# Hybrid encoder step on one core: projection begun inside its norm, gates spread over its tiles, FFN's first half turned between the second's products

## Chip, cores and metric

One core of a Trainium2 chip. The metric is the device time of the whole step in microseconds, of the one core that runs it. Every product is made in three passes of split float32 operands (high x high, high x low, low x high).

## What is computed

The reference, cut to what matters (x is 2048 prompt rows and 32 sample rows of 1024; D_FF is 2816):

```python
h = _rmsnorm(x, norm1_g)
z = h @ w_in                                   # 1024 x 3096
fq, fk, fv, fl, gq, gk, gv, gg, gr = split(z)  # 512 512 512 8 256 256 512 16 512
logf = log_sigmoid(fl + b_forget)
glog = log_sigmoid(gg @ w_gate2 + b_gate2) / 16
fox_o = softmax(fq.fk/8 + cumsum(logf) differences, causal) @ fv   # prompt; sample over 4096 cached rows
gla_o, S = gated linear attention in chunks (gq, gk, gv, cumsum(glog))
x = x + [fox_o, rmsnorm(gla_o) * silu(gr)] @ w_out
h = _rmsnorm(x, norm2_g)
x = x + (silu(h @ w_gate) * (h @ w_up)) @ w_down
y = _rmsnorm(x, final_norm_g)
```

## The kernel before

Each stage is a scope of its own with its SBUF tiles, semaphores and a barrier of all engines at its end: `project`, `gates`, `fox_prompt`, `fox_sample`, `gla`, `merge`, `ffn`. The engines' programs are written by hand, in order, one function per engine, with semaphores between them. Loads and stores go through SP's queue.

`project` (L133). The 2080 rows are 20 x tiles of 104. For each, ACT squares (L288) and takes the root (L292), DVE scales by its inverse and the gain (L348), PE turns eight 104x128 pieces (`turn_x`, L393), ACT copies the turned tile as high half (L297) and DVE subtracts it for the low half (L355). When all 20 are in `hT`, PE runs over 25 weight tiles of 128 columns: 8 column tiles, 16 row tiles and at the end the narrow one (8 forget gates and 16 gate ranks, run 128 wide). A weight tile takes 5 blocks of 416 rows, a block 24 products (8 depths x 3 passes, L405). ACT copies each block out (L314). Row tiles (k, v, GLA's v and its output gate) are turned back in groups of four 104-row pieces (`turn_rows`, L416): three groups after block 3, two after block 4, each after ACT's copy and before DVE's (L369). The column tiles are stored to `zT`, the row tiles to `new_k`, `new_v`, `zrow`.

`gates` (L452) begins when all that is stored. It reads the narrow tile back, makes the gate product (`gg @ w_gate2`, L552), takes min, Abs, Exp and Ln for the log sigmoids, sums along time with scans, sums the cached forget gates (L585 to L595), turns and stores `pbias`, `new_f`, `kbias`, `kb_split`, `gsum`. Nothing of the fox stage is loaded before its end.

`merge` (L1584) ends for each row tile with the second norm, whose turned rows `hT_m` are copied half by ACT (L1730), half by DVE (L1772) and stored as `h2T`.

`ffn` (L1832) takes the rows in two halves of 10 tiles (1040 rows, blocks of 4, 3 and 3 tiles). A half has 22 steps of 128 hidden columns; step u makes gate and up products of its columns (`gate_up`, 24 matmuls each per block, L2126) and, between them, the down products of the step before (`downs`, 12 matmuls a slot, six slots, L2141). DVE adds each down product to `yacc` (`adds`, L2061). The silu is exp on ACT (L2018), + 1, reciprocal and product on DVE (L2073 to L2077). ACT and POOL split the weights (L1998, L1957) and h (`hi_h`, `lo_h`, L2005, L1962; `hraw` holds two tiles). After a half's last down products, `final` (L2161, L2093, L2039, L2104) turns `yacc` back, adds x, norms and stores it, row tile by row tile, and POOL clears `yacc`; no product stands between.

Of the kernel before, what the change touches and what calls it, by code (L numbers as in the profile page):

```python
# [109 lines left out]
def fill_identity(pool, ident, filled):  # L110
# [10 lines left out]
TCOLS = [C_Q + P * n for n in range(4)] + [C_GQ + P * n for n in range(4)]  # L121
RCOLS = ([C_K + P * n for n in range(4)] + [C_V + P * n for n in range(4)]
         + [C_GV + P * n for n in range(4)] + [C_GR + P * n for n in range(4)])
NTT, NTR = len(TCOLS), len(RCOLS)
NWT = NTT + NTR + 1
R_Q, R_GQ, R_GK, R_K, R_F, R_GG = 0, 512, 768, 1024, 1536, 1544
XB = 4
NB = 5
BLK = NTOK // NB
TPB = BLK // TT  # L130


def project(nc, d):  # L133
    with ExitStack() as ctx:
# [4 lines left out]
        work = sb("work", [P, SEQ])  # L139
        xn = work[0:TT].rearrange("p (b c) -> p b c", b=2)  # L140
        zhi = work[:].bitcast(F32R)
        zlo = sb("zlo", [P, SEQ])
# [7 lines left out]

        xin = zs[0:TT].rearrange("p a t -> p (a t)")[:, 0:XB * D].rearrange("p (b c) -> p b c", b=XB)
        zr = sb("zr", [TT, NT, P])
        ps = psum("ps_project")
        x_in = [sem(f"x_in{b}") for b in range(XB)]
# [13 lines left out]
        def half_tile(n):  # L168

            return n if n < 4 else n - 4  # L170

        X_CREDIT = 2
        B_CREDIT = 2 * NB
        R_CREDIT = 2

        @block.sync
        def _(sp):
            for b in range(2):
                sp.sem_inc(t_stored[b], 16)
            sp.sem_inc(r_stored, 48)  # L180
            sp.sem_inc(halves_stored, 32)
            w = d["w_in"][0].rearrange("(k p) n -> p k n", p=P)

            def load_w(n):
# [3 lines left out]
                if n < NTT + NTR:  # L188
                    c = (TCOLS + RCOLS)[n]
                    sp.dma_start(wraw[:, b], w[:, :, c:c + P]).then_inc(w_come[b], 16)  # L190
# [4 lines left out]
            def load_x(t, b):  # L195
                sp.wait_ge(x_scaled, t + 1)
                sp.dma_start(xin[:, b], d["x_prompt"][0, bass.ds(t * TT, TT), :]).then_inc(x_in[b], 16)

            sp.dma_start(grow[:], d["norm1_g"].partition_broadcast(TT)).then_inc(g_in, 16)
            with sp.Fori(0, NT // XB - 1) as i:  # L200
                for b in range(XB):
                    load_x(XB * i + b, b)
            load_w(0)
            load_w(1)
            for b in range(XB - 1):
                load_x(NT - XB + b, b)

            sp.wait_ge(x_scaled, NT)
            sp.dma_start(xin[0:LAST_PROMPT, XB - 1], d["x_prompt"][0, (NT - 1) * TT:SEQ, :]).then_inc(x_in[XB - 1], 16)
            sp.dma_start(xin[LAST_PROMPT:TT, XB - 1], d["x_sample"][0]).then_inc(x_in[XB - 1], 16)  # L210

            def store_t(n, row, rows):
                sp.wait_ge(block_out, NB * (n + 1) + B_CREDIT)
                sp.dma_start(d["zT"][row:row + rows, :], zs[0:rows, n % 2]).then_inc(t_stored[n % 2], 16)

            def store_halves(n):
                part, j = divmod(half_tile(n), 4)
                sp.wait_ge(z_hi, half_tile(n) + 1)
                sp.dma_start(d["qk_hi"][part, j * P:(j + 1) * P, :], work[:]).then_inc(halves_stored, 16)
                sp.wait_ge(z_lo, half_tile(n) + 1)  # L220
                sp.dma_start(d["qk_lo"][part, j * P:(j + 1) * P, :], zlo[:]).then_inc(halves_stored, 16)

            def store_rows(n, prompt, sample, c):
                sp.wait_ge(rows_out, NB * (n - NTT + 1) + R_CREDIT)
# [10 lines left out]
            for n in range(NWT):  # L235
                if 1 <= n < NWT - 1:
                    load_w(n + 1)
# [379 lines left out]

# [1601 lines left out]
```

## Time and profile before

| | |
|---|---|
| runs | 3607.22, 3610.07, 3612.82 us; median 3610.07 |
| profiled execution | 3611.11 us, its span 3609.4 us |
| busy of the span | PE 3170.2 (88%), DVE 2241.3 (62%), ACT 1091.2 (30%), POOL 538.3 (15%) |
| mean granted clock of TensorE | 0.934 of full |
| chain that ended last, by line | PE L2126 27%, PE L2141 13%, loads of `yo` and `hraw` 2% |

The stages in time: norm and projection 0 to 700 us, gates to 768, fox prompt to about 1250, fox sample to about 1380, GLA to about 1670, merge to 1961, FFN to the end. Busy shares are averages over stages; what a change in a stage is worth is read from that stage. The time of the profiled execution is 1.7 us more than its span.

### The profile page before, as it was taken

The numbers are of one execution on the slowest core, as the hardware profiler recorded it, in microseconds if no ns is written. First come the engines' busy times: TensorE is split into PE (matmuls) and PEld (weight loads), VectorE is DVE, ScalarE is ACT, GpSimd is POOL, SyncE is SP. The second block draws the span as 40 slices with busy tenths as digits, with TensorE's granted clock in tenths as the row PEclk, the third lists the DMA queues.
The fourth block names the chain that finished last, engine by engine and source line by source line (L and its number), as shares of the span: only waits on it lengthen the run. The fifth ranks groups of instructions, "written<-read, shape, count | busy, mean of one in ns | idle before, by whom it ended". The sixth has DMA issues, their size and how long they took to land. (4 is left out here: it accounts for less than half of the span.)

```text
span 3609.4 us, 51369 instructions
## 1 busy us (share of the span) xinstructions
PE 3170.2 (88%) x19096; PEld 2924.1 (81%) x19096; DVE 2241.3 (62%) x3638; ACT 1091.2 (30%) x2163; POOL 538.3 (15%) x371
## 2 busy tenths in 40 slices
PE   5999999839999765664996999999997799999996
PEld 4999999728778644553774999999997799999995
DVE  5102111159999734995343678778776778778776
ACT  5211111138888622663222211111112211111112
POOL 0000000000000003661001322222124122222120
PEclk9999999859999976776998999999999899999997
DMA  4424312153342161222443311111112411111112
GB/s 111 164 71 160 104 53 70 31 110 65 71 95 53 31 217 40 83 80 94 127 142 125 90 46 46 41 46 46 46 56 78 119 46 44 43 46 46 46 48 81
DMA packets 249539, 281.24 MB, mean 78 GB/s; under 512 B 37729, under 2 KB 207089, under 8 KB 240137
## 3 DMA queue, kind: packets, MB, share of 16 engines
q1 hardware_dynamic: 248105, 275.71, 26.1%
q10 hardware_dynamic: 1344, 4.36, 0.6%
q8 instruction: 53, 0.87, 0.1%
q14 instruction: 37, 0.30, 0.0%
HBM read 196.33 MB, written 83.70 MB: 78 GB/s over the span
## 5 line engine op out<-in xcount | busy, mean ns | idle before, releaser
L2126 PE MATMUL ps_ffn<-h,wsp_n 128*128 128x312 f32 (+1 forms) x6336 | 1056.5, 323 | 42.2 <-POOL h L1962 29.5
L2126 PEld LDWEIGHTS ps_ffn<-h,wsp_n 128*128 128x128 f32 x6336 | 1017.4, 189 | 48.4 <-issue 38.4
L2061 DVE TENSOR_TENSOR yacc<-ps_ffn,yacc 128x312 f32<-128x312 f32 (+1 forms) x1056 | 495.2, 515 | 221.5 <-PE ps_ffn L2141 221.5
L405 PE MATMUL ps_project<-hT,wsp 128*128 128x416 f32 x3000 | 579.4, 353 | 3.2 <-DVE wsp L362 3.2
L405 PEld LDWEIGHTS ps_project<-hT,wsp 128*128 128x128 f32 x3000 | 561.4, 189 | 12.0 <-issue 5.0
L2141 PE MATMUL ps_ffn<-aT,dsp 128*128 128x312 f32 (+1 forms) x3168 | 545.0, 321 | 9.4 <-DVE yacc L2061 9.4
L2141 PEld LDWEIGHTS ps_ffn<-aT,dsp 128*128 128x128 f32 x3168 | 508.5, 188 | 12.2 <-issue 9.4
L2028 ACT ACTIVATE aT<-a 128x416 fp32r<-128x416 f32 x132 | 65.4, 495 | 1003.9 <-DVE a L2083 1003.9
L1957 POOL TENSOR_TENSOR wsp_n<-wraw_n,wsp_n 128x1024 fp32r<-128x1024 f32 x88 | 210.6, 2394 | 802.9 <-ACT wsp_n L1998 802.9
L2075 DVE RECIPROCAL silu<-silu 128x416 f32<-128x416 f32 x132 | 306.2, 2320 | 4.6
L2073 DVE TENSOR_SCALAR silu<-silu 128x416 f32<-128x416 f32 x132 | 221.9, 1681 | 49.9 <-ACT silu L2018 49.9
L1801 PE MATMUL ps_merge<-wsp_m,mT 128*104 128x512 f32 x960 | 227.9, 396 | 0.0
L941 DVE TENSOR_TENSOR pt<-ps_fox,pt 128x512 fp32r<-128x512 f32 (+1 forms) x320 | 194.5, 608 | 30.2 <-ACT pt L899 23.9
L362 DVE TENSOR_TENSOR wsp<-wraw,wsp 128x1024 fp32r<-128x1024 f32 x25 | 30.6, 1226 | 288.9 <-ACT wsp L305 288.9
L893 ACT ACTIVATE pexp<-ps_fox,ntop 128x512 f32<-128x512 f32 (+2 forms) x320 | 198.7, 621 | 36.2 <-DVE ntop L936 34.4
L1801 PEld LDWEIGHTS ps_merge<-wsp_m,mT 128*104 128x104 f32 x960 | 160.5, 169 | 58.8
L899 ACT ACTIVATE pt<-ps_fox 128x512 fp32r<-128x512 f32 (+1 forms) x320 | 171.0, 535 | 75.2 <-PE ps_fox L855 70.2
L928 DVE TENSOR_REDUCE tops<-ps_fox 128x1 f32<-128x512 f32 (+3 forms) x288 | 177.5, 617 | 26.2 <-PE ps_fox L821 24.9
L855 PE MATMUL ps_fox<-ident_f,pexp 128*128 128x128 f32 x1088 | 174.5, 276 | 2.3 <-DVE pt L941 1.6
L820 PE MATMUL ps_fox<-ka,qa 128*128 128x512 f32 (+2 forms) x320 | 127.2, 398 | 52.9 <-DMA kb<-kb_split 45.8
L1978 POOL TENSOR_TENSOR dsp<-draw,dsp 128x1024 fp32r<-128x1024 f32 x44 | 105.0, 2388 | 360.8 <-ACT dsp L2025 360.8
L855 PEld LDWEIGHTS ps_fox<-ident_f,pexp 128*128 128x128 f32 x1088 | 129.4, 144 | 26.7 <-DVE pt L941 5.8
(218 smaller groups left out, 3452.0 us busy)
## 6 DMA issues: line engine op xcount, KB each, us to landing
wraw_n<-in_w_gate_dram SPq DMA_DIRECT2D x44, 512.0 KB, 3.9
wraw_n<-in_w_up_dram SPq DMA_DIRECT2D x44, 512.0 KB, 3.8
draw<-in_w_down_dram SPq DMA_DIRECT2D x44, 512.0 KB, 3.6
zT<-zs SPq DMA_DIRECT2D x12, 1040.0 KB, 3.9
wraw<-in_w_in_dram SPq DMA_DIRECT2D x24, 512.0 KB
x<-x2s SPq DMA_DIRECT2D x20, 416.0 KB
h2T<-hT_m SPq DMA_DIRECT2D x20, 416.0 KB
hraw<-h2T SPq DMA_DIRECT2D x20, 416.0 KB
```

What stands on the lines that cost most here:

```text
L405: last = pe.matmul(ps[:, g, 0:BLK], wsp[:, b, s, k, :], hT[:, g * TPB:(g + 1) * TPB, v, k, :], start=m == 0, stop=m == 3 * KD - 1)
L855: last = pe.transpose(ps[:, turn_bank(u, j), q * P:(q + 1) * P], pexp[:, x, (j % NG) * P:(j % NG + 1) * P], ident[:])
L893: act.activation(pexp[:, n % PEXP, 0:w], ps[:, n % RING, 0:w], ACT.Exp, bias=ntop[:, u % 2, k:k + 1], accum_out=sums[:, u % 4, k, c:c + 1] ...
L928: dve.reduce_max(tops[:, k % 2, c:c + 1], rows, AX.X).then_inc(topped, 1)
L941: dve.tensor_tensor(pt[:, LO, m % 3, q0:512], ps[:, turn_bank(u, j), q0:512], pt[:, HI, m % 3, q0:512].bitcast(F32), ALU.subtract).then_in ...
L1801: last = pe.matmul(ps[0:TT, 2 + 2 * b + n, :], mT[:, b, s, k, :], wsp[:, v, k, n * 512:(n + 1) * 512], start=m == 0, stop=m == 3 * KD - 1)
L1957: pool.tensor_tensor(wsp[:, par, s, LO], wraw[:, s], wsp[:, par, s, HI].bitcast(F32), ALU.subtract).then_inc(gu_lo, 1)
L2061: dve.tensor_tensor(y, ps[:, 4 + i, 0:FB[b] * TT], y, ALU.add).then_inc(added, 1)
L2073: dve.tensor_scalar(x, x, 1.0, None, ALU.add).then_inc(one_done, 1)
L2075: dve.reciprocal(x, x).then_inc(inv_done, 1)
L2126: last = pe.matmul(ps[:, 2 * q + s, 0:FB[b] * TT], wsp[:, par, s, w, k, :], h2[:, FB0[b]:FB0[b + 1], v, k, :], start=m == 0, stop=m == 3 * ...
L2141: last = pe.matmul(ps[:, 4 + i, 0:FB[b] * TT], dsp[:, par, w, c:c + P], aT[:, par, x, cols(b)], start=m == 0, stop=m == 2)
```

## The change

Three stages are rewritten: `project`, which takes in all of `gates`, the end of `merge`, and `ffn`.

**Projection.** The narrow tile comes first and is 24 wide. A list `BLOCKS` fixes the order of the 125 blocks, five PSUM banks go round; from x tile 5 on, half a block (12 matmuls) follows each x tile's turns. x has three buffers in place of four, its first load goes ahead of the gain row, and turns and copies go by half tiles. Row groups are turned two blocks behind theirs (`ROW_LAG`), one group after each block.

**Gates.** Their work is given out over the slots after the tenth block, e = 0, 1, ...: the cache's sums at e = 0 to 8, the forget gates at e = 11 to 17, and ten units of up to 512 rows of GLA's gates at the slots in `G_AT`. They share bank 7. Their loads and stores are issued by POOL. POOL also makes the low halves of the first two weight tiles.

```diff
+BLOCKS = [(n, g) for g in range(NB) for n in range(2)] + [(n, g) for n in range(2, NWT) for g in range(NB)]
+NBLK = len(BLOCKS)
+X_LAG = 5
+ROW_LAG = 2
+
+GUNITS = [(g, 512 * j, min(512, NTOK - 512 * j)) for g in range(2) for j in range(5)]
+G_AT = [10, 12, 15, 17, 20, 22, 24, 27, 29, 31]
...
+            def gate(k):
+                g, tok, L = GUNITS[k]
+                pe.wait_ge(p_b_in, 48)
+                pe.wait_ge(p_z_in, 16)
+                if k == 0:
+                    pe.wait_ge(s_out, 8)
+                else:
+                    pe.wait_ge(p_g_abs, k)
+                if k == 2:
+                    pe.wait_ge(f_rows, 3)
+                pe.matmul(ps[:, 7, 0:L], wg2[:, g * P:(g + 1) * P], gg[:, tok:tok + L], start=True, stop=True).then_inc(gate_done, 1)
+
+            i = 0
+            for t in range(NT):
+                turn_x(t)
+                if t >= X_LAG:
+                    products(i // 2, i % 2)
+                    i += 1
+            while i < 4 * NB:
+                products(i // 2, i % 2)
+                i += 1
+            for p in range(2 * NB, NBLK + ROW_LAG):
+                if p < NBLK:
+                    products(p)
+                e = p - 2 * NB
+                if e == 0:
+                    later_sums()
+                if 1 <= e <= 8:
+                    turn_past(e - 1)
+                if e == 14:
+                    turn_f()
+                if e in G_AT:
+                    gate(G_AT.index(e))
+                m, h = BLOCKS[p - ROW_LAG]
+                if m >= N_ROWS:
+                    turn_rows(m, h)
...
+            for p in range(2 * NB, NBLK):
+                n, g = BLOCKS[p]
+                if g == 0 and n + 1 < NWT:
+                    hi_w(n + 1)
+                out(p)
+                e = p - 2 * NB
+                if e == 11:
+                    soft_f()
+                if e == 16:
+                    high_f()
+                if e - 1 in G_AT:
+                    soft_g(G_AT.index(e - 1))
+                if g == NB - 1 and N_Q <= n < N_K + 4:
+                    hi_half(n)
```

**Merge.** ACT copies the whole turned tile (832 columns) as the high half, then DVE subtracts it for the low half; `h2T` holds both, twice the bytes.

```diff
+                dve.wait_ge(h_high, t + 1 + CREDIT)
+                part = lambda s: hT[:, b, s].rearrange("p (a k) t -> p a (k t)", a=2)
+                dve.tensor_tensor(part(LO), ps[:, 6:8, 0:4 * TT], part(HI).bitcast(F32), ALU.subtract).then_inc(h_low, 1)
```

**FFN.** h is loaded split, straight into `h2`; the second half's blocks are loaded as the first half's last `up` product of that block is done. The + 1 of the silu is ACT's (Identity with a bias of ones). The first adds of a half are copies, so nothing is cleared. The first half's rows are turned in half rows of 512 columns, by the table `ROWS`, between the products of steps 22 and 23, all through bank 7; down products use three banks there. The final norm's square, root and scale are ACT's, its gain is POOL's. The second half's rows stand between and behind the last down products in banks 0 to 3; x has five buffers and, at the end, three spare ones.

```diff
+ROWS = {(NF, GU, 2): (0,), (NF, DN, 2): (1,), (NF, GU, 3): (2,), (NF, DN, 3): (3,),
+        (NF, GU, 4): (4,), (NF, DN, 4): (5,), (NF, GU, 5): (6,), (NF, DN, 5): (7,),
+        (NF + 1, GU, 0): (8,), (NF + 1, DN, 0): (9,), (NF + 1, DN, 1): (10,), (NF + 1, GU, 2): (11, 12, 13),
+        (NF + 1, DN, 2): (14,), (NF + 1, GU, 3): (15,), (NF + 1, DN, 3): (16,), (NF + 1, GU, 4): (17, 18, 19),
+        (STEPS, DN, 2): (0, 1), (STEPS, DN, 3): (2, 3), (STEPS, DN, 4): (4, 5, 6, 7), (STEPS, DN, 5): tuple(range(8, 2 * HT))}
+BATCHES = (((0, 1), (2, 3), (4,), (5, 6), (7, 8, 9)), ((0, 1), (2, 3), (4, 5), (6, 7), (8, 9)))
+NB2 = len(BATCHES[0])
...
-                        dve.tensor_scalar(x, x, 1.0, None, ALU.add).then_inc(one_done, 1)
...
+                        act.activation(x, x, ACT.Identity, bias=ones[:]).then_inc(one_done, 1)
...
+            def rows(u, kind, slot):
+                half = 0 if isinstance(u, int) and u < STEPS else 1
+                for r in rows_at(u, kind, slot):
+                    t, second = divmod(r, 2)
+                    g = half * HT + t
+                    if not second:
+                        pe.wait_ge(added, DGROUPS * (NF * (half + 1) - 1) + KD * (ffn_block(t) + 1) + ADD_CREDIT)
+                    if half and r == 0:
+                        pe.wait_ge(a_made, NFB * STEPS + A_CREDIT)
+                    pe.wait_ge(y_added, 2 * g + second + (0 if half == 0 else -3) + ROW_CREDIT)
+                    for c in range(4):
+                        last = pe.transpose(ps[0:TT, row_bank(half, r), c * P:(c + 1) * P],
+                                            yacc[:, 4 * second + c, t * TT:(t + 1) * TT], ident[:])
+                    last.then_inc(y_turned, 1)
```

The order of the instructions at three places. First PE in `project`, where the norm ends and the first slots begin; before, it is the norm's loop and the first column tile (`work` and `hT` are the scaled and the turned rows, `wsp` the split weights, `pos` at L654 the cache's sums). Before:

```order
L393 MATMUL ps_project<-ident,work 128x104 x8
L390 REGISTER_ALU
L391 REGISTER_ALU
L393 MATMUL ps_project<-ident,work 128x104 x8
L105 REGISTER_ALU
L105 COMPARE_AND_BRANCH
L435 UNCONDITIONAL_BRANCH
L435 ISA
L401 ISA
L405 MATMUL ps_project<-hT,wsp 128x416 x24
```

Now, from x tile 15 of 0 to 19 on:

```order
L616 MATMUL ps_project<-ident,work 128x104 x8
L629 MATMUL ps_project<-hT,wsp 128x416 x12
L616 MATMUL ps_project<-ident,work 128x104 x8
L629 MATMUL ps_project<-hT,wsp 128x416 x12
L616 MATMUL ps_project<-ident,work 128x104 x8
L629 MATMUL ps_project<-hT,wsp 24x416 x12
L616 MATMUL ps_project<-ident,work 128x104 x8
L629 MATMUL ps_project<-hT,wsp 24x416 x12
L616 MATMUL ps_project<-ident,work 128x104 x8
L629 MATMUL ps_project<-hT,wsp 128x416 x24
L629 MATMUL ps_project<-hT,wsp 24x416 x24
L629 MATMUL ps_project<-hT,wsp 128x416 x48
```

Two loops, turns alone and then products alone, have become one line in which 12 products stand between the turns of two x tiles.

Second ACT and the gates' functions (`fl`, `fbh` and `pos` before; `work`, `sa` and `pos` now). Before, in `gates`, after the whole projection:

```order
L524 UNCONDITIONAL_BRANCH
L529 ACTIVATE pos<-fl,bf 8x2080
L534 ACTIVATE pos<-ps_gates,bg 128x416 x10
L536 ACT_TABLE_LOAD
L536 ACTIVATE pos<-pos 8x2080
L537 ACTIVATE pos<-pos 128x4160
L539 ACT_TABLE_LOAD
L539 ACTIVATE pos<-pos,ones 8x2080
L540 ACTIVATE pos<-pos,ones 128x4160
L542 ACTIVATE fbh<-fb 8x2048
L453 UNCONDITIONAL_BRANCH
L884 UNCONDITIONAL_BRANCH
```

Now, between the copies of blocks (`zs`), from slot 10 on:

```order
L382 ACTIVATE zs<-ps_project 128x416 x2
L396 ACTIVATE work<-work,bf 8x2048
L397 ACTIVATE sa<-sa,bf 8x32
L399 ACT_TABLE_LOAD
L399 ACTIVATE work<-work 8x2048
L400 ACTIVATE sa<-sa 8x32
L402 ACT_TABLE_LOAD
L402 ACTIVATE work<-work,ones 8x2048
L403 ACTIVATE sa<-sa,ones 8x32
L414 ACTIVATE pos<-ps_project,bg 128x512
L416 ACT_TABLE_LOAD
L416 ACTIVATE pos<-pos 128x512
```

Behind the block of slot 11 ACT has six wide and narrow functions and two table loads, then the first unit's three with two more, before it copies another block.

Third PE in the FFN, step 22, the first of the second half; `yacc` is what is turned. Before:

```order
L2141 MATMUL ps_ffn<-aT,dsp 128x312 x12
L2126 MATMUL ps_ffn<-h,wsp_n 128x312 x24
L2141 MATMUL ps_ffn<-aT,dsp 128x312 x12
L2161 MATMUL ps_ffn<-ident_n,yacc 104x128 x80
L1881 UNCONDITIONAL_BRANCH
L1881 ISA
L2120 ISA
L2126 MATMUL ps_ffn<-h,wsp_n 128x416 x24
```

Now:

```order
L2308 MATMUL ps_ffn<-aT,dsp 128x416 x12
L2290 MATMUL ps_ffn<-h,wsp_n 128x312 x24
L2323 MATMUL ps_ffn<-ident_n,yacc 104x128 x4
L2308 MATMUL ps_ffn<-aT,dsp 128x312 x12
L2323 MATMUL ps_ffn<-ident_n,yacc 104x128 x4
L2290 MATMUL ps_ffn<-h,wsp_n 128x312 x24
L2323 MATMUL ps_ffn<-ident_n,yacc 104x128 x4
L2308 MATMUL ps_ffn<-aT,dsp 128x312 x12
L2323 MATMUL ps_ffn<-ident_n,yacc 104x128 x4
L2290 MATMUL ps_ffn<-h,wsp_n 128x312 x24
```

The 80 turns of `final` in one piece have become pieces of four (twice of twelve) between gate, up and down products.

## Rows read from the trace of the kernel before

**Rows 1.** Stretches: start:end us, length, busy us (x instructions) by engine, PEclk, DMA share, GB/s
```profile
0.00:71.48 71.48, 32.63 (x160) 26.58 (x161) 49.04 (x62) 48.40 (x84) 0.74 (x7) 1.00 0.51 140
71.48:696.40 624.92, 615.01 (x3320) 595.59 (x3320) 101.26 (x112) 98.34 (x155) 0.00 (x0) 1.00 0.29 93
696.40:767.51 71.11, 22.87 (x75) 11.19 (x74) 38.53 (x38) 23.41 (x19) 2.84 (x7) 0.57 0.17 44
1961.44:1983.01 21.57, 0.00 (x1) 0.03 (x1) 6.99 (x1) 5.68 (x6) 12.86 (x9) 0.50 0.48 147
2100.00:2600.00 500.00, 500.00 (x3162) 497.88 (x3161) 399.44 (x571) 83.30 (x132) 105.23 (x44) 1.00 0.16 46
2735.10:2826.70 91.60, 52.68 (x297) 48.65 (x296) 58.76 (x77) 29.09 (x51) 32.10 (x22) 0.78 0.43 129
```

**Rows 2.** Timeline of PE in the norm: start us, us, line, form, count [idle before <- releaser]
```profile
13.47 3.03 PE L393 MATMUL ps_project<-ident,work 104*128 104x104 f32 x16 [13.47 <-DVE work L348]
...
66.59 1.65 PE L393 MATMUL ps_project<-ident,work 104*128 104x104 f32 x8 [0.68 <-DVE work L348]
71.48 88.79 PE L405 MATMUL ps_project<-hT,wsp 128*128 128x416 f32 x457 [3.25 <-DVE wsp L362]
```

**Rows 3.** Timeline of PE over one row tile of the projection, same columns
```profile
595.14 18.47 PE L405 MATMUL ps_project<-hT,wsp 128*128 128x416 f32 x96
613.44 1.03 PE L416 MATMUL ps_project<-ident,zs 128*104 128x128 f32 x8
614.83 0.65 PE L416 MATMUL ps_project<-ident,zs 128*104 128x128 f32 x4 [0.35 <-DVE zr L369]
615.23 4.80 PE L405 MATMUL ps_project<-hT,wsp 128*128 128x416 f32 x24
619.87 0.60 PE L416 MATMUL ps_project<-ident,zs 128*104 128x128 f32 x4
...
621.31 18.48 PE L405 MATMUL ps_project<-hT,wsp 128*128 128x416 f32 x96
```

**Rows 4.** Timeline of several engines, end of the projection and gates, same columns
```profile
674.80 3.71 SPq L228 DMA_DIRECT2D zrow<-zr  x1
...
700.48 0.33 SPq L489 DMA_DIRECT2D gg<-zT  x1
...
705.11 7.30 PE L552 MATMUL ps_gates<-gg,wg 16*128 16x416 f32 x10 [8.71 <-DMA bf<-in_b_forget_dram]
...
724.56 1.28 ACT L536 ACT_TABLE_LOAD   x1
...
725.85 1.94 ACT L536 ACTIVATE pos<-pos 8x2080 f32<-8x2080 f32 x1
```

**Rows 5.** Timeline of PE at the start of the FFN, same columns
```profile
1983.01 18.05 PE L2126 MATMUL ps_ffn<-h,wsp_n 128*128 128x416 f32 x96 [26.65 <-POOL h L1962]
...
2005.85 13.96 PE L2126 MATMUL ps_ffn<-h,wsp_n 128*128 128x312 f32 x72 [4.79 <-DVE a L2083]
...
2019.65 2.42 PE L2141 MATMUL ps_ffn<-aT,dsp 128*128 128x416 f32 x12
```

**Rows 6.** Chain that ended last, late FFN: start us, us, what
```profile
2701.00 4.54 PE ps_ffn L2126 x24
...
2862.76 4.57 PE ps_ffn L2126 x24
...
3514.25 4.54 PE ps_ffn L2126 x24
...
3551.30 10.47 DVE yacc L2061 x24
...
3568.86 5.71 DMA yo<-x
```

**Rows 7.** Groups: line, engine, operation, form, count | busy us, mean ns | idle before
```profile
L1957 POOL TENSOR_TENSOR wsp_n<-wraw_n,wsp_n 128x1024 fp32r<-128x1024 f32 x88 | 210.6, 2394 | 802.9 <-ACT wsp_n L1998 802.9
...
L2039 ACT ACTIVATE ps_ffn<-yo 104x1024 f32<-104x1024 f32 x20 | 20.5, 1027 | 59.8 <-DVE yo L2093 59.8
```

More of the change, by code:

```diff
@@ new lines, in _ @@
+            done = 0
+            for t in range(NT + 1):
+                if t < NT:
+                    square(t)
+                if t in (1, 2):
+                    hi_w(t - 1)
+                if t:
+                    hi_h(t - 1)
+                while done < (t - X_LAG) // 2:
+                    out(done)
+                    done += 1
+            while done < 2 * NB - 1:
+                out(done)
+                done += 1
+            hi_w(2)
+            out(2 * NB - 1)
+            act.wait_ge(filled, 7)
@@ L1978, in step, with last @@
                     pool.tensor_tensor(dsp[:, par, LO], draw[:], dsp[:, par, HI].bitcast(F32), ALU.subtract).then_inc(d_lo, 1)
[L1979 to L1989 removed]
+                if mid is not None:
+                    for t in (range(0, 2), range(5, 7), range(7, HT))[mid]:
+                        gained(t)
+            def last():
+                for t in range(HT, NT):
+                    gained(t)
+            steps(pool, prelude, step, last)
         @block.scalar
         def _(act):
[L1993 removed]
+            act.wait_ge(filled, 4)
             def hi_gu(u, par, s):
@@ L2009, in prelude, with square, root @@
                     hi_gu(0, 0, s)
-                for b in range(NFB):
-                    hi_h(0, b)
-            def step(u, par, off, gu, down, between=None):
+            def square(half, t):
+                act.wait_ge(y_added, 2 * (half * HT + t) + 2 + ROW_CREDIT)
+                act.wait_ge(squared, half * HT + t)
+                act.activation(junk[:], rows_of(half * HT + t), ACT.Square, accum_out=msq[:, t:t + 1]).then_inc(squared, 1)
+            def root(half, k):
+                ts = BATCHES[half][k]
+                act.wait_ge(squared, half * HT + ts[-1] + 1)
+                act.activation(rms[:, ts[0]:ts[-1] + 1], msq[:, ts[0]:ts[-1] + 1], ACT.Sqrt, scale=1.0 / D, bias=eps[0:TT]).then_inc(rooted, 1)
@@ new lines, in scale @@
+            def scale(half, k):
+                act.wait_ge(inverted, half * NB2 + k + 1)
+                for t in BATCHES[half][k]:
+                    y = rows_of(half * HT + t)
+                    act.activation(y, y, ACT.Copy, scale=inv[:, t:t + 1]).then_inc(y_scaled, 1)
+            def rows(u, kind, slot):
+                half = 0 if isinstance(u, int) and u < STEPS else 1
+                for r in rows_at(u, kind, slot):
+                    t, second = divmod(r, 2)
+                    if second:
+                        square(half, t)
+                        k = batch_of(half, t)
+                        if t == BATCHES[half][k][-1]:
+                            root(half, k)
+                            if half:
+                                scale(half, k)
+                if isinstance(u, int) and (u, kind, slot) in SCALES:
+                    scale(0, SCALES[u, kind, slot])
@@ L2168, in _ @@
-            steps(pe, lambda: None, step, True, final)
+                        downs(u, 1 - par, slot)
+                    rows(u, DN, slot)
+            steps(pe, lambda: None, step, lambda: None)
 SCRATCH = {
@@ L2193, in stream_step @@
     project(nc, d)
-    gates(nc, d)
     fox_prompt(nc, d)
```

1053 lines of the change are left out of this document (548 added, 505 removed).

## Prediction

> **What bounds the kernel now.** I read the stages first, as stretches of one table [rows 1]. PE is busy for 615 of the 625 us of the projection's products and for all of the FFN's steady stretch, both at clock 1.00. The gain can only come from stretches where PE is not full: the norm in front of the projection (32.6 of 71.5 us), the gates (22.9 of 71.1, clock 0.57), the wait before the FFN's first product (none of 21.6) and the FFN's change of halves (52.7 of 91.6, clock 0.78). The change works on all four. The FFN's steady steps stay as they are: 34.29 us each, from two starts 19 steps apart [rows 6]. DVE has 399 of 500 us there, so what is taken from DVE buys nothing.
>
> The measuring rod is the profiled execution, 3611.1 us (span 3609.4); the median of the runs is 1.0 us lower. About 0.2%, 7 us, is what a measurement can tell from no change.
>
> **1. Products inside the norm.** Norm and turns take one tile in 2.80 us, the first turned at 13.47 and the twentieth at 66.59; products start at 71.48 [rows 2]. In the change, x tiles 5 to 19 are each followed by 12 products, half a block. A block of 24 lasts 4.64 us from start to start [rows 3], so a half is 2.3 us; eight turns take at most 1.65 us [rows 2], less when the next operands are there. PE then needs about 3.6 us a tile. ACT and DVE have 48.4 and 49.0 us of work in 20 tiles [rows 1], 2.4 us each, to which 0.5 us of copies a tile comes; that fits under it. The first five tiles still take about 3 us each. With the first x tile now loaded ahead of the gain row (about 1.5 us earlier), the last half ends near 12 + 16 + 15 x 3.6 = 82 us. Then 7.5 blocks are done, 34.5 us of work: (71.5 + 34.5) - 82 = **-24 us**. Ends: -30 if the turns hide, -5 if a tile takes 5 us.
>
> **2. Row turns one slot late.** In a row tile PE spends 621.31 - 595.14 less 120 products, 26.17 - 23.0 = 3.2 us on 20 turns. It includes waits for DVE's and ACT's copies (the 0.35 before 614.83) and the loop's registers. Twelve turns there take 1.44 us without the wait, 0.48 for four [rows 3]. Now each four stand two slots behind their block, when the copies are long done: 5 x 0.48 = 2.4. 16 x 0.8 = **-12 us** (ends -6, -18: 0.40 to 0.55 for four).
>
> **3. Gates.** The stage runs from 700.48 to 767.51 [rows 4]: **-67 us** go. Into the projection's PE line come ten gate products of 4160 columns (the first 2080 took 7.30 us at the lower clock, so 7.3 for all at the higher) and 53 small turns at 0.12: **+13 us**. One wait is in sight. The second gate product, slot 12 after the tenth, waits for ACT's first absolute value, which stands behind the forget gates' Abs, Exp and Ln over 2048 (1.94 each) with two table loads of 1.28 [rows 4] and small ones: 9.0 us, begun when slot 11 ends, against one slot of 4.6 us. PE loses 5 to 6: **+6 us**. ACT's block copies queue behind it too, until 14 us after slot 11; five banks cover four slots, 18 us, so no product waits. Later units need some 4.5 us of ACT (two table loads each) in 2.3 slots of 4.6, and hide. Transfers for them go by POOL's queue; if one is late, the next unit's Abs is, then PE's gate product. **The end:** before, a narrow tile closed the stage, and its last product ended 4.1 us before 700.48. Now a row tile does: copy, turn, copy (2 us), then three stores, whose two small ones hold SP for 3.7 and about 1.7 us [rows 4], then landing: about 11 us, **+7 us**. The fox stage's start (17 us of loads) is unchanged. Together -41; ends -50 and -20 (each of the ten units holding PE 2 us more).
>
> **4. The merge writes h split.** ACT copies 832 instead of 416 columns, DVE subtracts 832 after it instead of copying 416 beside it. Inside, PE's work per tile is longer than either's. Behind the last tile ACT's 0.4 more, DVE's 1.0 (1.03 us per 1024 columns [rows 7]) and the landing of twice the bytes (1.4 at 306 GB/s) add up: **+3 us** (2 to 5).
>
> **5. The FFN's start.** First product at 1983.01, step 1's second slot at 2019.65: 36.6 us for 168 products, with a wait of 4.8 at 2005.85 because ACT was still splitting h [rows 5]. Now h comes split, 8.5 MB instead of 4.3. In the stretch before the first product 147 GB/s moved with the DMA engines 0.48 busy [rows 1], 306 if full: 1 MB of weights and block 0's 3.4 MB land 14.4 us after the first bytes, so PE starts near 1977. Without the wait the second slot comes at 2009: **-11 us**. Blocks 1 and 2 need 8.4 us each where PE takes 9 and 7. Step 1's weights queue behind all h (3 us each) and are ready near 2001, before 2004. Ends: -13; +25 if the rate stays at 147 (block 0 in 23 us, each next in 17, step 1's weights in 10).
>
> **6. The change of halves.** Step 21 starts at 2701.00, step 24 at 2862.76 [rows 6]: 161.8 instead of 3 x 34.29, a loss of **58.9 us**. Now the 20 half rows stand between products of steps 22 and 23. Four turns 0.5: 10 us. Bank 7 is their only one, and in the two triples the second and third wait for DVE's add and back (24 adds in 10.47 us [rows 6], so 0.44 for 347 columns and 0.65 for 512): 4 x 1.2, 5 us. Three banks for the down products: 2 us. ACT squares, takes five roots, and each brings two table loads (2.6 us) ahead of an Exp; DVE then is late, and PE with it, once in a while: 7 us. New loss 24, so **-35 us** (ends -48 and -15). DVE's load in those steps stays below PE's (11 more adds, less three tensor_scalars). h for the second half is loaded as each block's last product frees it, a step ahead.
>
> **7. The tail.** Adds 3551.30 to 3561.77, then to the end ten rows in rounds of DVE, SP and reload. Now rows begin between the adds, and ACT (square and scale 1.03 each, and what stands between) and POOL (2.39 for 1024 columns) [rows 7] need about 25 us for ten. But tiles 18 and 19 reuse buffers of 13 and 14: a store that lands in some 4 us, a reload of 5.7 [rows 6]; the second lands near 3588, then add, square, root, scale, gain and store: 3603 against 3609.4. **-7 us** (ends 0, -14).
>
> Step work: +1 moves from DVE to ACT as Identity. The built order has no table load between it and Exp, and ACT is busy 83 of 500 us: nothing. The Trainium skill (ScalarE: Activation LUTs, "Table sets: the hidden batching unit") puts identity, copy and abs into every set, which is the reason; a reload per Exp would be 2.6 us in three blocks a step, 7.7 us more for ACT. No row shows Identity itself.
>
> **Sum:** -24 -12 -67 +13 +6 +7 +3 -11 -35 -7 = -127, less 1 for the median: 3611 - 128 = about **3483 us**.
>
> **Rivals.** (A) The changed halves stay dear: squares and table loads in ACT's in-order line hold Exp back in every block of two steps, and 6 gives 15: 3503. For: ACT waits there for PE and DVE in turn. Against: a step leaves ACT 28 us. 0.15. (B) The projection's slots wait: each gate unit's round (gate product, min, Abs, Exp, Ln, scan, store) is longer than its slots, 3 us each: 3513. For: each begins only when the one before is stored. Against: 11.6 us a unit, 7 to 8 of work. 0.12. (C) The products starve the norm: the turns come late, a tile takes 5 us, the first term is -5: 3502. 0.08. (D) h comes at 147 GB/s, the end of term 5: 3519. Against: the low share came from two buffers waiting for ACT and POOL. 0.05. (E) **Slower**: the POOL queue's transfers are slow. A unit has some 11.6 us, 6 of it work, so a store beyond 5 us is PE's wait, ten times over. To eat 127 us a store of 256 KB must take 18 us. Nothing in the profile is issued by POOL; before, 2 MB of the same sums were stored and landed within 8 us before 767.51. 0.03 (0.02 slower, 0.01 near nothing).
> The Trainium skill (SBUF — State Buffer, "A bandwidth-pool intuition that's wrong") has a rule against such transfers: the descriptors are written by GpSimd, which a two-port VectorE operation locks out until it ends. By it each transfer would be late by one DVE operation of its slot, a few us; the sum would hardly move, the rounds would come to their slots' edge. No row here shows it.
>
> **Numbers.** The forecast has 0.57. Several ends at once are rare; the range 3460 to 3515 takes in A to D and some 23 us of better luck (turns, halves and gates at their good ends). Faster 0.97, same 0.01, slower 0.02.
>
> **What would show it.** PE's products start near 28 us instead of 71; no stage between projection and fox, whose first load is issued near 690; one PE wait of 5 to 6 us at the second gate product; first FFN product 15 us after the stage's first load; step 22 to 24 in about 93 us; steps of 34.29 elsewhere. Steps that lengthen, or waits at each gate product, would prove it wrong.

## The result and the profile after

The changed kernel takes **3478.7 us** (median of 4 runs, 3476.4 to 3480.5) against 3611.5 (4 runs, 3607.2 to 3613.5) of the kernel before: ratio 0.963, 95% interval 0.962 to 0.965. The forecast was 3483, with a range of 3460 to 3515. The profiled executions have spans of 3476.2 and 3609.4 us, 133.2 apart, and the table below divides these.

Where the stages lie now, as stretches of the changed kernel (columns as in [rows 1]):

```profile
0.00:76.44 76.44, 55.74 (x328) 41.83 (x329) 47.46 (x78) 51.83 (x110) 7.39 (x18) 1.00 0.52 135
76.44:672.50 596.06, 590.38 (x3218) 565.05 (x3217) 141.32 (x170) 151.34 (x210) 12.98 (x22) 0.99 0.33 101
672.50:684.93 12.43, 1.65 (x13) 1.18 (x11) 1.98 (x3) 0.52 (x1) 0.00 (x0) 0.68 0.35 86
684.93:1883.57 1198.64, 949.96 (x5878) 755.83 (x5878) 806.88 (x1650) 613.26 (x1416) 171.86 (x193) 0.88 0.36 102
1883.57:1898.40 14.83, 0.00 (x0) 0.03 (x1) 0.00 (x0) 3.40 (x3) 5.20 (x6) 0.50 0.95 349
2000.00:2500.00 500.00, 500.00 (x3156) 497.85 (x3155) 331.33 (x525) 108.21 (x175) 103.96 (x44) 1.00 0.16 46
2643.33:2735.13 91.80, 82.61 (x514) 79.39 (x513) 58.32 (x97) 46.19 (x65) 30.11 (x13) 0.94 0.36 110
3389.55:3476.20 86.65, 56.52 (x368) 54.20 (x367) 47.24 (x89) 30.80 (x47) 25.73 (x11) 0.84 0.28 76
```

The norm ends in products (76.44); the gates' stage of 67 us is gone; from the FFN's first load to its first product 349 GB/s move instead of 147; the two steps of the change of halves have PE busy for 82.6 of 91.8 us. DVE has 331 us of work in 500 where it had 399 [rows 1], and PE has no more than before.

PE in three places, the end of the norm, the first gate units and the row tiles (timeline: start, us, line, form, count, [idle before and what ended it]):

```profile
75.79 0.88 PE L616 MATMUL ps_project<-ident,work 104*128 104x104 f32 x8
76.44 18.41 PE L629 MATMUL ps_project<-hT,wsp 128*128 128x416 f32 x96
...
144.09 1.12 PE L676 MATMUL ps_project<-zr 16*128 16x512 f32 x2
145.14 9.37 PE L629 MATMUL ps_project<-hT,wsp 128*128 128x416 f32 x48
160.19 2.04 PE L676 MATMUL ps_project<-zr 16*128 16x512 f32 x2 [5.68 <-ACT pos L414]
162.16 10.66 PE L629 MATMUL ps_project<-hT,wsp 128*128 128x416 f32 x48
172.76 1.13 PE L661 MATMUL ps_project<-ident,zlo 8*104 8x8 f32 x19
...
287.25 0.60 PE L641 MATMUL ps_project<-ident,zs 128*104 128x128 f32 x4
287.61 4.80 PE L629 MATMUL ps_project<-hT,wsp 128*128 128x416 f32 x24
292.25 0.60 PE L641 MATMUL ps_project<-ident,zs 128*104 128x128 f32 x4
```

The last half product begins at 76.44, with 7 blocks done. Of ten gate units only the second makes PE wait, for 5.68 us; behind the wait the granted clock of 160 to 173 us is 0.81, so that 48 products last 10.66 instead of 9.37 us. A row slot (a block of 24 products and the four turns behind it) is 5.00 us, of which the four turns take 0.40 beside a bare block of 4.60 (24 of 1056 products in 202.27 us before).

Term by term, each from the start of one thing to the start of the next in both traces:

| step of the forecast | forecast | measured | between |
|---|---|---|---|
| 1 products in the norm | -24 | -27.5 | 76.44 with 7 blocks done against 71.48 + 7 x 4.64 |
| 2 row turns a slot late | -12 | -18.4 | 16 tiles of 25.02 against 26.17 |
| 3 gates | -41 | -36.7 | the rest up to the first load of attention: 684.93 against 767.51 |
| attention and GLA | 0 | -0.4 | up to the merge's first load, 1586.62 and 1669.62 |
| 4 merge | +3 | +5.1 | up to the FFN's first load, 1883.57 and 1961.44 |
| 5 start of the FFN | -11 | -14.0 | up to the second slot of step 1, 1927.75 and 2019.65 |
| steady steps | 0 | 0.0 | up to step 21: 681.34 and 681.35 |
| 6 change of halves | -35 | -32.8 | steps 21 to 43: 780.46 and 813.25 |
| 7 tail | -7 | -8.5 | from step 43 (3389.55 and 3514.25) to the end |
| sum | -127 | -133.2 | |

Six kernels with the same code up to the FFN reach its first load between 1880.96 and 1883.57, so about 2 us of such a difference (in the merge's row, say) mean nothing.

### The profile page after: what moved, and what is told of

Its sections match the earlier page's. It is cut to its first block and busy times, and to the rows that moved or that the text cites. A ratio compares the mean times of both kernels' runs of the same rounds, so it can differ in the third digit from the quotient of the medians.

```text
span 3476.2 us, 50599 instructions
## 1 busy us (share of the span) xinstructions
PE 3133.6 (90%) x19097; PEld 2887.6 (83%) x19097; DVE 2027.8 (58%) x3535; ACT 1207.3 (35%) x2345; POOL 556.0 (16%) x388
## 5 line engine op out<-in xcount | busy, mean ns | idle before, releaser
L2216 DVE TENSOR_TENSOR yacc<-ps_ffn,yacc 128x312 f32<-128x312 f32 (+1 forms) x1008 | 488.0, 519 | 388.3 <-PE ps_ffn L2308 388.3
L629 PE MATMUL ps_project<-hT,wsp 128*128 128x416 f32 (+1 forms) x3000 | 600.7, 356 | 0.0
L629 PEld LDWEIGHTS ps_project<-hT,wsp 128*128 128x128 f32 (+1 forms) x3000 | 546.2, 185 | 23.9 <-issue 8.7
L485 DVE COPY zr<-ps_project 104x512 f32<-104x512 f32 x80 | 55.2, 692 | 300.6 <-PE ps_project L641 175.6
L382 ACT ACTIVATE zs<-ps_project 128x416 f32<-128x416 f32 (+1 forms) x125 | 64.5, 516 | 443.7 <-PE ps_project L629 443.7
L2179 ACT ACTIVATE silu<-ps_ffn 128x416 f32<-128x416 f32 x132 | 60.7, 460 | 296.2 <-PE ps_ffn L2290 296.2
```

The lines of the kernel that those rows point to most:

```text
L629: last = pe.matmul(ps[0:w, p % NB, 0:BLK], wsp[:, b, s, k, 0:w], hT[:, g * TPB:(g + 1) * TPB, v, k, :], start=k == 0 and m == 0, stop=k == ...
L2216: dve.tensor_tensor(y, z, y, ALU.add).then_inc(added, 1)
```

## The experiments

All are the changed kernel with one edit, if nothing else is said; where an edit has more places than are shown, `...` stands for them. Where a gain is a few us, I read the stage that was edited, and the medians beside it. Two spreads bound what such readings can tell. The kernel before, run beside these kernels, had medians of 3610.8 us (1, 2, 3 and 5), 3611.1 (4, 6, 8 and 10) and 3609.8 (7, 9 and 11), against 3611.5 beside the changed kernel: up to 1.7 us of a difference of medians may not be the edit's. And the six traces in which nothing between steps 22 and 43 was edited (the changed kernel's and those of 1, 2, 3, 8 and 9) need 745.9 to 749.1 us for them, the changed kernel 746.2.

**1. No products in the norm** (late_products)

```
-X_LAG = 5
+X_LAG = 40
```

> The changed kernel (3478.7 us) with one number other: the 30 half products no longer stand between the turns of x tiles 5 to 19, all products come behind the last turn. Everything else (gates in the slots, turns two slots late) stays. My theory: the first 15 half products give what the changed trace shows, 27.5 us (last half begins at 76.44 with 7 blocks done, against 71.48 with none before); so about 3506, and the first product near 70 us. Rival: the norm in the changed kernel is slower or faster for other reasons (x loaded first, three banks for the turns), and the products beside it give only a part, say 15 us: about 3494.

Measured: 3497.5 us (3495.1 to 3498.0), 18.7 more, between the two. PE's timeline around the last turn:

```profile
58.56 1.65 PE L616 MATMUL ps_project<-ident,work 104*128 104x104 f32 x8 [0.75 <-DVE work L463]
61.48 1.65 PE L616 MATMUL ps_project<-ident,work 104*128 104x104 f32 x8 [1.27 <-DVE work L463]
62.82 47.43 PE L629 MATMUL ps_project<-hT,wsp 128*24 128x416 f32 x245
```

Products start at 62.8 us here, 71.5 in the kernel before [rows 2]. So term 1 is two things: a norm that is 8.7 us faster by itself (first turn at 11.1 instead of 13.5; tiles of 2.57 instead of 2.80 us; products 1.3 us behind the last turn, not 4.9), and 18.8 us for the products within.

**2. Turns bunched as before** (turns_bunched)

```
-ROW_LAG = 2
+ROW_LAG = 0
...
+def rows_due(p):
+    n, g = BLOCKS[p]
+    return [(n, h) for h in {3: (0, 1, 2), 4: (3, 4)}.get(g, ())] if n >= N_ROWS else []
...
-                m, h = BLOCKS[p - ROW_LAG]
-                if m >= N_ROWS:
+                for m, h in rows_due(p):
                     turn_rows(m, h)
```

> The changed kernel with the row turns in the order of the kernel before: three fours behind a tile's fourth block, two behind its fifth, instead of one four behind each block, two slots late. Same 80 fours. My theory: what the change gained there is the two waits and the restarts of a bunch, 1.2 us a tile (26.17 before, 25.02 now), so 16 x 1.2 = 18 us come back: about 3497, with row tiles of 26.2 us and waits of 0.35 and 0.25 us for DVE's and ACT's copies. Rival: the gain came from the loops that were written out (no registers and branches between tiles), and the order is worth little: within 3 us of 3479.

Measured: 3492.5 us (3490.0 to 3496.7), 13.7 more; the first load of attention comes at 700.64 instead of 684.93, 15.7 later. One tile of PE:

```profile
317.95 1.03 PE L646 MATMUL ps_project<-ident,zs 128*104 128x128 f32 x8
319.49 0.62 PE L646 MATMUL ps_project<-ident,zs 128*104 128x128 f32 x4 [0.51 <-DVE zr L491]
...
325.27 0.65 PE L646 MATMUL ps_project<-ident,zs 128*104 128x128 f32 x4 [0.17 <-ACT zs L388]
...
343.99 1.04 PE L646 MATMUL ps_project<-ident,zs 128*104 128x128 f32 x8
```

343.99 - 317.95 is 26.04 us, with both waits back, and 25.02 with the turns spread: 16 x 1.02 = 16 of the 18.4 us are the order, nearer to what I expected (3497) than to the rival. The other 2 are left for the loops that were written out, by difference alone; no run has only them.

**3. The first gate unit ahead of the forget gates** (unit_first)

```
+                if e - 1 in G_AT:
+                    soft_g(G_AT.index(e - 1))
                 if e == 11:
                     soft_f()
...
-                if e - 1 in G_AT:
-                    soft_g(G_AT.index(e - 1))
...
                 if e == 12:
+                    low_g(1)
                     log_f()
```

> The changed kernel with ACT's work behind slot 11 in another order: the first gate unit's Abs, Exp and Ln stand ahead of the forget gates' three, and DVE takes the second unit's minimum ahead of the forget gates' subtraction. My theory: PE's wait of 5.7 us at the second gate product goes, with the 2.2 us that the 48 products and the gate product behind it lost at a lower granted clock; the small turns of the forget gates then wait some 1.7 us for DVE. So 6 us less: 3472 to 3473. Rival: the forget gates' chain is what is late, and the wait only moves to the small turns at slot 14: 3478, no gain.

Measured: 3472.8 us (3471.3 to 3474.2), 5.9 less, as expected. On PE:

```profile
153.81 1.12 PE L677 MATMUL ps_project<-zr 16*128 16x512 f32 x2
154.86 9.37 PE L630 MATMUL ps_project<-hT,wsp 128*128 128x416 f32 x48
165.89 1.13 PE L662 MATMUL ps_project<-ident,zlo 8*104 8x8 f32 x19 [1.65 <-DVE sn L524]
...
167.01 6.34 PE L630 MATMUL ps_project<-hT,wsp 128*128 128x416 f32 x24
```

The second gate product no longer waits. The small turns wait 1.65 us instead, and the 24 products behind them take 6.34 us, not 4.82, at a granted clock of 0.77: the low clock costs about as much as the wait before it.

**4. The new projection alone** (front_only)

The kernel before with the changed `project` in the place of `project` and `gates`.

> The kernel before with only the projection and gates of the changed kernel; merge and FFN are those of before, h unsplit. My theory: the stages are separate, and what the changed trace shows up to the first load of the attention stage, 82.3 to 82.6 us, is the whole of this part: 3611 - 82.5 = 3528 to 3529, and the other 50 us belong to merge and FFN. Rival: part of the later gain hangs on the first part (the order of loads, clock at the stage's start), or the attention stage runs slower behind it: off by 5 us or more.

Measured: 3531.0 us (3528.2 to 3533.4), 80.1 less than the 3611.1 of its comparison; the first load of attention is at 684.51, 83.0 earlier. So this part gives what it gave in the whole change, and the stages behind it run as before within 3 us.

**5. 1 + exp(-x) back on DVE** (one_on_dve)

```
-                        act.activation(x, x, ACT.Identity, bias=ones[:]).then_inc(one_done, 1)
+                        dve.tensor_scalar(x, x, 1.0, None, ALU.add).then_inc(one_done, 1)
```

> The changed kernel with the FFN's 1 + exp(-x) back on DVE, as in the kernel before (132 more operations of DVE, as many fewer of ACT). My theory: nothing in the steady steps, where PE has no gap, so within 3 us of 3478.7, perhaps 1 to 3 us more at the change of halves, where DVE's line is full. Rival: with the rows of the first half in the steps, DVE is what PE waits for there, and each of six blocks costs 0.5 us and more: 3483 to 3487.

Measured: 3483.5 us (3483.0 to 3485.3), 4.8 more: the size of the rival, but not its place. Steady steps are the same (PE busy for 500.00 of 500 us). The loss is at the FFN's start: 3.9 us from its first load to step 21, which five traces with the operation on ACT pass within 0.4 us of each other. Steps 22 to 43 take 747.9 us, inside the spread of the traces without this edit, so a loss in the changed halves isn't shown. All executions of the operation (count: shortest/median/longest ns, first and last start, forms):

```profile
L2256 DVE TENSOR_SCALAR silu<-silu x132: 300/1890/2503, 1904.2 to 3423.5; 128x312 f32<-128x312 f32 x88, 128x416 f32<-128x416 f32 x44
```

PE, DVE and POOL at the FFN's start, timelines:

```profile
1924.35 6.35 PE L2290 MATMUL ps_ffn<-h,wsp_n 128*128 128x416 f32 x24 [2.39 <-DVE a L2267]
...
1916.08 2.52 DVE L2269 TENSOR_TENSOR aT<-a,aT 128x416 fp32r<-128x416 f32 x1 [7.20 <-ACT aT L2190]
1918.53 2.50 DVE L2256 TENSOR_SCALAR silu<-silu 128x312 f32<-128x312 f32 x1
...
1925.13 0.31 DVE L2256 TENSOR_SCALAR silu<-silu 128x312 f32<-128x312 f32 x1
...
1915.76 5.09 POOL L2095 TENSOR_TENSOR wsp_n<-wraw_n,wsp_n 128x1024 fp32r<-128x1024 f32 x2 [22.82 <-ACT wsp_n L2136]
```

The same operation takes 0.31 us alone and 2.50 where POOL subtracts; it ends when POOL's does (1921.0 and 1920.9), and the median of 132 is 1.89 us. PE then waits 2.39 us, and its next 24 products last 6.35 us, where the next 24 of their size (at 1932.79) last 4.70: wait and low clock together come to 4.0, the size of the loss. The subtraction before it (`aT`, both inputs in SBUF) is held in the same way by the first of POOL's two, 2.52 us where its median is 0.48; that one is in the changed kernel too. The Trainium skill (SBUF — State Buffer, "Who interferes with whom") says that a tensor_scalar of DVE can take the port pair that it shares with GpSimd, and that the later of the two then waits for the whole of the other's instruction. The trace agrees.

**6. Weights ahead of the stores** (weights_ahead). In step 23, ahead of three groups of four turns that stand together (11, 12 and 13 of `ROWS`), PE waits 5.71 us for DVE's addition of a half row. What stood behind it, in timelines of SP, ACT and PE of the changed kernel, with the stretch behind the wait in the columns of [rows 1]:

```profile
2694.91 0.39 SPq L2024 DMA_DIRECT2D wraw_n<-in_w_gate_dram  x1
...
2700.41 1.06 ACT L2136 ACTIVATE wsp_n<-wraw_n 128x1024 fp32r<-128x1024 f32 x1 [10.45 <-DMA wraw_n<-in_w_gate_dram]
...
2704.01 0.53 ACT L2192 ACTIVATE aT<-a 128x416 fp32r<-128x416 f32 x1
...
2705.83 1.09 PE L2323 MATMUL ps_ffn<-ident_n,yacc 128*104 128x128 f32 x4 [5.71 <-DVE yo L2228]
...
2705.83:2715.00 9.17, 7.51 (x31) 6.61 (x32) 4.02 (x8) 8.51 (x12) 6.85 (x3) 0.51 0.39 104
```

SP issues step 24's weights behind two stores and two reloads; ACT's line waits 10.45 us for them; DVE waits for ACT's `aT`, and the addition stands behind that. The wait isn't all of the cost: for 9.2 us behind it the granted clock is 0.51, 12 down products of 312 columns last 3.47 us and not 2.12, and such differences add up to some 3.5 us.

```
+                early = (NF + 2, NF + 3, NF + 4)
+                if not is_last(u) and not (isinstance(u, int) and u + 1 in early):
...
+                if isinstance(u, int) and u + 2 in early:
+                    load_gu(u + 2, u + 2 - off)
                 if isinstance(u, int) and u in (NF, NF + 1, NF + 2):
```

> The changed kernel, FFN, SP's queue alone: the gate and up weights of steps 24, 25 and 26 are issued before the stores and reloads of steps 22, 23 and 24, not behind them (two steps of the second loop are written out on SP for that). My theory: the wait of 5.7 us in the triple of turns in step 23 comes from SP. It stood in the stores of tiles 0 and 1 and issued step 24's weights only at 2694.9; ACT's line waited for them until 2700.4, and behind it stood the square, the root and the activation's half that DVE and PE wait for. The 2.65 us wait of step 25 is the same thing after the stores of tiles 7 to 9. Both go, with the 1 to 2 us that low clock costs behind the first: 8 to 10 us less than 3478.7, so about 3470. Rival: ACT's table loads and the x rows' reloads are as late, and the triple waits for DVE's row 10 in any case: 3 us less, 3476.

Measured: 3474.0 us (3472.3 to 3475.4), 4.7 less; steps 22 to 43 (2642.11 to 3386.67) take 744.6 us, only 1.7 less than in the changed kernel and 1.3 less than in any of the six traces. The wait is gone from the three groups that stand together, and a longer one stands behind them (PE):

```profile
2700.20 0.62 PE L2329 MATMUL ps_ffn<-ident_n,yacc 128*104 128x128 f32 x4 [0.87 <-DVE yo L2234]
...
2715.85 1.09 PE L2329 MATMUL ps_ffn<-ident_n,yacc 128*104 128x128 f32 x4 [7.85 <-DVE yo L2234]
```

and SP's queue at that place:

```profile
2704.92 0.37 SPq L2027 DMA_DIRECT2D wraw_n<-in_w_up_dram  x1
2705.34 0.56 SPq L2052 DMA_DIRECT2D out_y_p_dram<-yo  x1
2710.87 0.33 SPq L2047 DMA_DIRECT2D yo<-x  x1
```

The cause of the wait was right and the price of the edit wrong: SP now stands at the up weights until POOL has freed their buffer (2704.9), and tile 2, ready at 2700.2, is stored behind them; its buffer is back for tile 7 5 us late.

**7. Weights between the stores** (weights_between)

```
+                if isinstance(u, int) and u in (NF, NF + 2):
+                    load_gu(u + 2, u + 2 - off)
...
+                        if t == 3:
+                            load_gu(NF + 3, 3)
```

> As weights_ahead, but step 25's gate and up weights stand between the stores and reloads of tiles 2, 3 and those of tiles 4 to 6, not ahead of all. In weights_ahead SP stood at the up weights until POOL had done with the tiles' products (2704.9), and tile 2, ready at 2700.2, was stored 5 us late, so its buffer came back late for tile 7, and PE waited 7.85 us there (turn behind the triple). My theory: the store goes at once, the reload lands 5 us earlier, that wait falls to 3 us, and the weights still come in time: 3469 to 3470. Rival: the wait for tile 7 is the buffer's own round (add, root, scale, product by the gain, store 5.5, reload 4.1), whatever SP does first: 3474, as weights_ahead.

Measured: 3472.0 us (3471.2 to 3473.8), 6.7 less than the changed kernel (5.0 beside the kernel before, which ran 1.7 us faster here) and between what I expected (3469 to 3470) and the rival; step 22 to 43 in 742.0 us, 4.2 less and 3.9 below the lowest of the six traces. The store goes at 2700.06, x for tile 7 is there for the addition at 2708.03, and PE waits 0.96 us. What is left is 4.18 us at 2723.04, for x of tile 9, whose buffer's store went behind the weights and let the reload go only at 2718.04, and four waits of 0.8 to 1.6 us. So a round of a buffer and the weights still share SP.

**8. Two more places for x at the tail** (five_spares)

```
+            if in_yacc(g):
+                c = 2 * TT * (g - NT + 2)
+                return yacc[0:TT, :, c:c + P]
...
+                for t in range(NT - 2, NT):
+                    load_x(t)
                 for t in range(HT, NT):
                     store(t)
-                    if t in (HT + 3, HT + 4):
-                        load_x(t + YB)
```

> The changed kernel, its tail: x of tiles 18 and 19 goes into columns of yacc that are already turned, not into the buffers of tiles 13 and 14 behind their stores. My theory: the end of the chain (store 5.1, reload 4.5, adds, square, root, scale) goes, and POOL's products by the gain set the end: six more at 2.35 us behind the pair that ended at 3449.2, so the last ends near 3463.3 instead of 3469.1. 6 us less: about 3473. Rival: ACT's line (square 1.15, scale 1.1 and a root of 0.3 and more a tile) or DVE's turn to turn wait for the four banks is as slow, and it ends within 2 us of now: 3477.

Measured: 3470.9 us (3468.8 to 3472.3), 7.8 less; from step 43 to the end 80.2 instead of 86.65 us. The chain, piece by piece:

```profile
3452.19 1.16 ACT junk L2159 x2
...
3453.37 0.30 ACT rms_n L2164
...
3454.96 1.13 ACT draw L2170
3456.09 1.05 ACT junk L2159 x2
...
3457.22 1.16 ACT junk L2159 x2
...
3458.93 1.16 ACT yacc L2170
...
3460.16 2.35 POOL yacc L2118
```

The size came as expected, but the bound is ACT (square, square, root, two scales: 5.03 us a pair of rows, from 3452.19 to 3457.22), not POOL.

**9. The tail's rows shared** (tail_shared): five_spares, with

```
+                    dve.scalar_tensor_tensor(out=y, in0=y, scalar=inv[:, t:t + 1], in1=as_row(grow[:], HT + t),
+                                             op0=ALU.mult, op1=ALU.mult).then_inc(y_done_v, 1)
```

> five_spares, and DVE takes the scale and the gain of every second row of the tail in one operation (1.3 us in the kernel before), in the place of ACT's scale (1.13) and POOL's product (2.35). The trace of five_spares has ACT's squares and scales end to end, 5.03 us for each two tiles from 3442 to 3459, POOL's last product behind them. My theory: ACT then needs 3.7 us for two tiles and DVE 3.9, so four pairs save 4 to 5 us, and the last row saves POOL's 2.35 less 1.3: 5 us less than five_spares (3470.9), about 3466. Rival: DVE's operation, ahead of the next adds, holds PE's turns and ACT's squares back by what it saves: 3470.

Measured: 3469.4 us (3468.6 to 3473.2), 1.6 less than five_spares, of which 1.3 could be the two comparisons' own; the tail itself takes 78.9 us against 80.2. The rival: DVE's operation stands between additions that ACT's squares wait for, and a pair takes 4.3 us (squares at 3444.45 and 3448.75) instead of 5.0.

**10. Edits 3, 6 and 8** (all_three)

> The changed kernel with the three edits together: the first gate unit ahead of the forget gates' functions (5.9 us measured), the weights of steps 24 to 26 ahead of the stores, and the two more places for x at the tail. They are in three stages, so the gains should add up: 5.9 + 8 + 6 = 20 us, about 3459. Rival: they do not add, since what one frees the next wait takes: 3465 or more.

Measured: 3463.4 us (3461.1 to 3466.3, 5 runs), 15.3 less, between the two: the singles' 5.9, 4.7 and 7.8 add to 18.4, of which the stages themselves showed 1.7 for the second and 6.5 for the third. Step 22 to 43 is 744.56 us, as in weights_ahead.

**11. Everything** (best): edits 3, 7, 8, 9, and the small turns one slot later (`if e == 15: turn_f()`, with `G_AT = [10, 12, 16, 18, ...]`).

> All edits together: the first gate unit first, with the small turns of the forget gates one slot later and the third and fourth unit one slot later each (so that neither the 1.65 us wait nor the 1.5 us of low clock behind it comes), the weights between the stores, five more places for x, the tail's rows shared by ACT with POOL and DVE. Theory: 3478.7 - 5.9 - 3.2 - 9 - 7.8 - 5 = about 3448. Rival: two of the three FFN edits don't give what they should, or not beside each other: 3456 or more.

Measured: **3453.9 us** (3453.1 to 3455.2, 5 runs), ratio to the kernel before 0.957 (0.955 to 0.958), 24.9 less than the changed kernel (23.2 if each is taken beside its own runs of the kernel before), between the 3448 that I expected and the rival's 3456. Its steps 22 to 43 take 741.5 us and its tail 78.9, as in weights_between and tail_shared. Between the first product behind the norm and the last of the projection PE waits for nothing any more:

```profile
168.05 1.13 PE L662 MATMUL ps_project<-ident,zlo 8*104 8x8 f32 x19
...
169.17 4.82 PE L630 MATMUL ps_project<-hT,wsp 128*128 128x416 f32 x24
```

24 products behind the small turns take 4.82 us again: without the wait the clock does not fall.

## Why the prediction was right, and where it was not

- **1, products in the norm** (-24; -27.5). "A tile 3.6 us" is 3.4 (6.83 for two), and the last half ended near 79, not 82. What the step did not see is that 8.7 us of the gain are the norm's own, not the products'; the run without products (1) shows it. I had counted 1.5 us of this, for the first load.
- **2, row turns** (-12; -18.4, just past the good end, -18). I priced four turns at 0.48 us and they take 0.40: with 80 groups that is the whole difference of 6.4. The bunched order put back 1.02 us a tile.
- **3, gates** (-41; -36.7). The place and size of the wait (5 to 6 us at the second gate product) were right, 5.68. Two terms were too small: behind the wait the lower clock took 2.2 us, and the tail from the last product to the first load of attention is 12.4 us, not 11. PE's own work was 14 us, not 13. Rival B was wrong: nine of ten units made no wait, though ACT waited for the store of the unit before, 11.9 us in five waits.
- **4, merge** (+3; +5.1, of which some 2 are within the spread of traces). I gave DVE's rate by a row of ACT's (1.03 us per 1024 columns [rows 7]). No run isolates this part, and where the 2 us are stays open.
- **5, start of the FFN** (-11; -14.0, just past the good end). PE starts 14.8 us after the first load, where the forecast had some 15.5. I took the rate if the DMA engines were full as 306 GB/s; it was 349. Rival D is out. The rest is a cost that I left in: I took the wait of 4.8 us out of the 36.6, but not the low clock behind it. The kernel before has a granted clock of 0.59 there, in the columns of [rows 1]:

```profile
2005.85:2012.00 6.15, 6.15 (x27) 6.15 (x28) 4.38 (x6) 2.40 (x5) 2.48 (x2) 0.59 0.39 107
```

The 168 products took 31.8 us of PE there and take 29.4 now, 2.5 less. That no wait came in its place is the work of the operation moved to ACT.

- **"+1 as Identity: nothing"** was the one step that was wrong in kind. I priced it by steady steps, where DVE has slack, and 0 is right there. At the FFN's start PE waits for DVE, and the operation lasts 1.9 to 2.5 us beside POOL's subtraction, not 0.3. Moving it is worth 4.8 us by the medians, 3.9 of them inside term 5; what it gives at the change of halves isn't shown. That Identity brings no table load was right: in the changed kernel's step 22 it starts 0.46 us behind its Exp and takes 0.56 us. DVE's 399 us were the hint: some 44 such operations (3 in each step of 34.29) are the 68 us that are gone from 500, so 1.6 us each.
- **6, change of halves** (-35; -32.8, of which -35.7 up to step 24). The new loss up to step 24 is 23 us as forecast (24), but that is luck in part. "ACT's table loads hold Exp back, once in a while", 7 us, was the wrong cause: SP, which issues weights behind stores and reloads, cost 5.7 us of wait and some 3.5 of low clock behind it. The waits for bank 7 came to 3.3 us and not 5, and the three banks to 0.2 and not 2. A last wait of 2.65 us in step 25, after the stores of tiles 7 to 9, was not in the forecast at all. I had followed each transfer by itself, and not what stands behind a waiting SP. This last wait has a second part (DVE, POOL and PE):

```profile
2791.46 2.41 DVE L2269 TENSOR_TENSOR aT<-a,aT 128x416 fp32r<-128x416 f32 x1 [7.27 <-ACT aT L2192]
...
2791.07 5.06 POOL L2095 TENSOR_TENSOR wsp_n<-wraw_n,wsp_n 128x1024 fp32r<-128x1024 f32 x2 [16.73 <-ACT wsp_n L2136]
...
2794.32 1.99 PE L2308 MATMUL ps_ffn<-aT,dsp 128*128 128x312 f32 x12 [2.65 <-DVE yacc L2216]
```

The weights that came late free DVE's and POOL's subtractions almost at once, and DVE's, 0.59 us otherwise, takes 2.41.

- **7, tail** (-7; -8.5). The reloads of tiles 18 and 19 ended last, as said; taking them away gave 6.5 us there.
- **Rivals A and C** are out: the changed halves lost 23 us and not 44, and a tile of the norm took 3.4 us and not 5.
- **Rival E, slower**: the POOL queue's stores of 256 KB landed 3.4 us after issue in the median, far from 18. The rule of the Trainium skill that I set beside it (SBUF — State Buffer, "A bandwidth-pool intuition that's wrong") speaks of DVE locking GpSimd out. These stores show no such delay; one load of 1 KB in that queue took 7.5 us to land, and why stays open. It was the other direction, DVE behind POOL, that cost time, in experiment 5.

The errors have both signs (3.5, 6, 3 and 1.5 us better, 4, 2 and 2 worse), and the sum is off by 6 for the spans and 4 for the medians: the total is nearer than its terms because they cancel.

## What to carry to other kernels

When stores and weight loads share one in-order queue, ask for each wait of the queue what stands behind it: here a store that waited for a product, and not its own duration, delayed weights, and through ACT's line the additions and PE. Price an operation that moves between engines in every stage in which someone waits for the engine, not in the steady one alone. And a PE wait costs more than itself, since products behind it ran at a lower clock: 2.2 us behind a wait of 5.68 in the projection, some 3.5 behind one of 5.71 in the FFN, 1.5 behind one of 1.65.

## What the runs showed that I had not expected

- DVE's tensor_scalar from SBUF to SBUF lasts 0.31 us alone and until POOL's two-input subtraction ends otherwise (median 1.89 of 132). A DVE subtraction with both inputs in SBUF did the same where it met POOL's (2.4 to 2.5 us; median 0.48).
- A PE wait of 1.65 us was enough for a granted clock of 0.77 over the 7.4 us behind it, 1.5 us lost; one of 5.68 us lost 2.2, and one of 5.71 us some 3.5 at a granted clock of 0.51.
- With h loaded straight to its place, no engine in between, the loads of the FFN's start moved 349 GB/s over 14.8 us, with the DMA engines at 0.95, and 417 in the next 8.6 us.
